# Layer norms taken apart by token chunk and woven into the blocks before and after them

## The chip, the cores and the metric

The kernel runs on one NeuronCore of a Trainium2 chip. The metric is the device time of one launch in microseconds (us). Five engines work side by side, each in its own program order: TensorE (PE in the profile) multiplies matrices, VectorE (DVE) and ScalarE (ACT) do elementwise work, GpSimd (POOL) and SyncE (SP) do the rest. They wait for one another through counting semaphores: `wait_ge(s, n)` holds an engine until `s` has reached `n`, and `.then_inc(s, 1)` raises `s` when an instruction has finished. A waiting engine runs nothing that stands behind the wait.

## The reference, cut to what matters

A two-layer decoder trunk works on 1024 prompt tokens and 8 sample tokens with a model width of 1024. Layer 0 has a Mamba-2 mixer, layer 1 a differential attention; each is followed by a squared-ReLU MLP, and after each of the four a layer norm closes the residual.

```python
def layer_norm(x, g, b):
    mu = jnp.mean(xf, -1, keepdims=True)
    var = jnp.mean(jnp.square(xf - mu), -1, keepdims=True)
    return ((xf - mu) * lax.rsqrt(var + LN_EPS) * g + b)

def sq_relu_mlp(x, w_up, w_down):
    return jnp.square(jax.nn.relu(x @ w_up)) @ w_down

for layer in range(2):
    y = mamba2_mixer(x, ...) if layer == 0 else diff_attention(x, ...)
    x = layer_norm(DN_ALPHA * x + y, ln_g[layer, 0], ln_b[layer, 0])
    x = layer_norm(DN_ALPHA * x + sq_relu_mlp(x, ...), ln_g[layer, 1], ln_b[layer, 1])
```

## The kernel before, in words

**Layout.** Activations lie transposed: 128 partitions hold one tile of features, 8 tiles (`k`) make the width of 1024, and the 1032 tokens run along the free dimension, cut into three token chunks (`c`) of 344. `acc` is the residual in float32. A matrix operand is kept as a high and a low part (`xh`/`xl`, `wh`/`wl`, `hh`/`hl`, `yh`/`yl`, `ah`/`al`), and a product is the sum of three matmuls.

**Jobs and units.** A job is one output tile of 128 features; its three chunks go into the three PSUM banks of `jb`. Weights come as units of 128x1024, loaded by SP and split by POOL into `wh` and `wl` in two slots. POOL may split into a slot once `unit_begun` shows that the unit that follows in the other slot has begun, for then the old one is finished. An ordinary `jobs` loop runs job by job and within it chunk by chunk, so a unit is used once and for one stretch. VectorE adds each finished bank to `acc` and frees it (`bank_free`); in the last block ahead of a layer norm (`accumulate_last`) it also sums the eight tiles into `ln0`, chunk by chunk of every job.

**The layer norm** has a part on three engines. PE: `mean` matmuls of `ln0` against a matrix of 1/1024 (line 493), then for each chunk the variance (24 small matmul instructions, line 499) and the spreading of the reciprocal roots over the partitions (6, line 506). DVE: centring (1316), the sum of the two halves of the squares (1320), the reciprocal (1324), scaling (1330), the low part (1337). ACT: squares (895), roots (899), the shifted high part (907). At the end DVE multiplies the residual by alpha in eight steps (1361). The order is written out by hand: all three means, then centre 0, centre 1, sum 0, centre 2 and so on, with two buffers for the squares (`lnq[:, c % 2]`). PE's order is variance and spread of chunks 0, 1 and 2, and only then the first matmul of the next stage (`jobs_after_norm`, line 532), which runs two jobs (`j` = 0, 1) chunk by chunk, 24 matmuls each, and waits for the low part of a whole chunk.

**After it.** In an MLP, ACT takes the relu out of a bank (942) and squares it (944), DVE squares it again and makes the low part (1373, 1375); there are four `rl` buffers, so the relu of the fifth chunk job waits for DVE's first (`h_ready`). After the second norm the first two jobs give query and key of head 0; DVE then forms lambda (from line 1399) and rotates them (1421) before the scores can begin (655).

**The four norms.** Norm 0 follows the mixer's last block (8 jobs of `yh`, two tiles deep, 6 matmuls a chunk job), norms 1 and 3 the last down block of an MLP (8 jobs, 12 matmuls a chunk job, 4 units), norm 2 the last attention projection (8 jobs, 3 matmuls a chunk job, one unit). After norm 3 the result is shifted and written out.

Of the kernel before, what the change touches and what calls it, by code (L numbers as in the profile page):

```python
# [110 lines left out]
def program(nc, a, o):  # L111
    with ExitStack() as ctx:
# [109 lines left out]
        m.close()  # L222

        m = ctx.enter_context(ExitStack())
        lnq = sb("lnq", [P, 2, KD, CW], F32, m)
# [87 lines left out]
        def _(pe):  # L313
# [170 lines left out]
            pe.wait_ge(s["y_lo"], 2 * GROUPS)  # L484
            jobs(Place(J_MLP0 - 8, U_MLP0 - 2), 8, 2, yh, yl)


            blocks = ((0, 0), (P, 0), (CW - P, 3 * P - CW))

            def layer_norm(l):  # L490
                for c in range(NCH):
                    pe.wait_ge(s["ln_sum"], 3 * l + c + 1)
                    mm(aux[:, c, 0:CW], ones[:, 0:P], ln0[:, c * CW:(c + 1) * CW], start=True, stop=True).then_inc(s["ln_mu"], 1)

                def variance(c):
                    pe.wait_ge(s["ln_add"], 3 * l + c + 1)
                    for b, (t0, _) in enumerate(blocks):
                        for k in range(4):
                            last = mm(aux[:, c, 500 + b:501 + b], lnq[:, c % 2, k, t0:t0 + P], ones[:, 0:1],  # L499
                                      start=(k == 0), stop=(k == 3))  # L500
                    last.then_inc(s["ln_var"], 1)

                def spread(c):
                    pe.wait_ge(s["ln_inv"], 3 * l + c + 1)
                    for b, (t0, skip) in enumerate(blocks):
                        last = mm(aux[:, c, t0 + skip:t0 + P], rstd[:, 1, 3 * c + b:3 * c + b + 1].to_broadcast([P, P]),  # L506
                                  ident[:, skip:P], start=True, stop=True)
                    last.then_inc(s["ln_scale"], 1)

                variance(0)  # L510
                spread(0)
                variance(1)
                spread(1)
                variance(2)
                spread(2)

            def jobs_after_norm(at, l):
# [3 lines left out]
                for c in range(NCH):  # L521
                    pe.wait_ge(s["ln_lo"], 3 * l + c + 1)
                    for j in range(2):
# [6 lines left out]
                        for k in range(KD):  # L530
                            for w, x, p in ((wh, xh, 0), (wh, xl, 1), (wl, xh, 2)):
                                last = mm(jb[:, bank, 0:CW], w[slot][:, k], x[:, k, cols],
                                          start=(k == 0 and p == 0), stop=(k == KD - 1 and p == 2))

                                if k == 0 and p == 0 and (c, j) in ((0, 0), (2, 1)):
                                    last.then_inc(unit_begun, 1)
                        last.then_inc(chunk_full, 1)

            def mlp(layer):
# [22 lines left out]
                down(at, 1, (hb + FFB) * 12)  # L562

            layer_norm(0)
            mlp(0)
            layer_norm(1)
# [8 lines left out]
            def project_head(at, n, new, fin):  # L575
# [51 lines left out]
                if fin:  # L627
# [96 lines left out]
            layer_norm(2)  # L724
            mlp(1)
            layer_norm(3)
# [3 lines left out]
        def _(act):  # L730
# [158 lines left out]
            def layer_norm(l):  # L889
                def squares(c, g):  # L890
                    act.wait_ge(s["ln_cent"], 6 * l + 2 * c + g + 1)
                    if c == 2:

                        act.wait_ge(s["ln_var"], 3 * l + 1)
                    af(lnq[:, c % 2, 4 * g:4 * g + 4], acc[:, 4 * g:4 * g + 4, c * CW:(c + 1) * CW], ACT.Square).then_inc(s["ln_sq"], 1)  # L895
# [31 lines left out]
                for c in (1, 2):  # L927
                    shift(c)

            def mlp(layer):  # L930
# [3 lines left out]
                def up(at, b, block_, order=UP_ORDER):  # L934
                    _, done = at.job(4)
                    for x, (j, c) in enumerate(order):
                        e = block_ * 12 + x

                        if not isinstance(e, int) or e >= 4:
                            act.wait_ge(s["h_ready"], e - 3)  # L940
                        act.wait_ge(chunk_full, done + x + 1)
                        af(rl[:, x % 4], jb[:, x % 3, 0:CW], ACT.Relu).then_inc(bank_free[x % 3], 1)  # L942
                        act.drain()
                        af(hh[b][:, j, c * CW:(c + 1) * CW], rl[:, x % 4], ACT.Square).then_inc(s["h_sq"], 1)  # L944

                up(Place(j0, 0), 0, hb, UP_ORDER_AFTER_NORM)
# [15 lines left out]
            layer_norm(0)  # L962
            mlp(0)
            layer_norm(1)
# [95 lines left out]
            for x, (j, c) in enumerate(UP_ORDER_AFTER_NORM[0:6]):  # L1060
                act.wait_ge(chunk_full, done + x + 1)
                af((raw, raw_k)[j][:, c * CW:(c + 1) * CW], jb[:, x % 3, 0:CW], ACT.Copy).then_inc(bank_free[x % 3], 1)
            act.drain().then_inc(s["raw_full"], 2)
# [15 lines left out]
            layer_norm(2)  # L1079
# [7 lines left out]
        def _(dve):  # L1087
# [51 lines left out]
            def accumulate_last(at):  # L1139

                for k in range(KD):
                    _, done = at.job()
                    for c in range(NCH):
                        cols = slice(c * CW, (c + 1) * CW)
                        dve.wait_ge(chunk_full, done + c + 1)
# [601 lines left out]
```

## Time and profile before

| | us |
|---|---|
| median of 3 runs (3884.25 to 3893.59) | 3885.5 |
| span of the profiled execution, first to last instruction | 3857.8 |
| TensorE busy in it | 3440.0 (89%) |
| VectorE / ScalarE / GpSimd busy | 2287.6 / 953.7 / 1011.1 |
| mean granted TensorE clock, share of full speed | 0.922 |

The profile is of one execution, and its span does not hold what lies around the first and last instruction, so the median stands 27.7 us above it. In timelines each row is a start, a length, the engine, the line of the kernel, the operation, what it writes and reads, its shape and how many instructions were merged; brackets tell how long the engine had been idle and whose work ended that.

### The profile page before, as it was taken

What the parts mean: (1) busy time and instruction counts of PE and PEld (TensorE: products, weight loads), DVE (VectorE), ACT (ScalarE), POOL (GpSimd) and SP (SyncE); (2) the same over time, 40 slices, a digit from 0 to 9 for tenths busy, and PEclk for the clock granted to TensorE, in tenths of its full rate; (3) what the DMA queues carried; (4) which work ended last, traced back from release to release, by engine and by line L of the source; (5) the groups of instructions that cost most, each with busy time, mean ns of one, the idle gap of its engine ahead of it and who ended that gap; (6) DMA issues with size and microseconds to landing.
All of it is one profiled execution on the core that took longest, in us unless ns stands there. A gap on an engine that the chain in (4) does not pass through costs nothing.

```text
span 3857.8 us, 55382 instructions
## 1 busy us (share of the span) xinstructions
PE 3440.0 (89%) x21050; PEld 3288.6 (85%) x21050; DVE 2287.6 (59%) x3463; ACT 953.7 (25%) x2235; POOL 1011.1 (26%) x455
## 2 busy tenths in 40 slices
PE   6888988889887899999997888888886799999997
PEld 6788888888787899999996787777775799999997
DVE  6677777777776834343457666666675753333335
ACT  3333333233332311111103323222322211111112
POOL 3123132222221233343431111111110043333331
PEclk9899999999998899999997888888897699999997
DMA  4231111111110011111112111211111011111111
GB/s 165 74 110 57 46 44 42 51 39 45 43 48 34 28 44 46 49 45 50 44 50 63 59 35 49 65 60 60 60 41 41 11 50 45 45 50 44 45 48 52
DMA packets 85936, 200.29 MB, mean 52 GB/s; under 512 B 8920, under 2 KB 46808, under 8 KB 85248
## 3 DMA queue, kind: packets, MB, share of 16 engines
q1 hardware_dynamic: 35552, 139.54, 10.8%
q10 hardware_dynamic: 50224, 58.37, 4.9%
q8 instruction: 131, 2.15, 0.2%
q14 instruction: 29, 0.24, 0.0%
HBM read 166.93 MB, written 39.60 MB: 54 GB/s over the span
## 4 chain that ended last, share of the span: by engine, by line
issue 65%; PE 19%; POOLq 9%; POOL 5%; SPq 1%; DVE 0%; ACT 0%; DMA 0%; ACTq 0%; DVEq 0%
PE jb L323 18%; POOLq L298 8%; POOL wl L299 5%; SPq L273 1%; PE aux L499 0%; DMA wraw<-in_wstream 0%; ACT acc L907 0%; DVE acc L1316 0%; POOLq L306 0%; POOLq L295 0%; SPq L263 0%; SPq L269 0%; DVE lnq L1320 0%; ACT lnq L895 0%; PE aux L506 0%
## 5 line engine op out<-in xcount | busy, mean ns | idle before, releaser
L296 POOL TENSOR_TENSOR wh<-wraw,one 128x1024 fp32r<-128x1024 f32 x225 | 444.5, 1976 | 2749.5 <-PE jb L323 2275.8
L323 PE MATMUL jb<-xh,wh 128*128 128x344 f32 x2784 | 912.7, 328 | 45.9 <-issue 18.6
L323 PE MATMUL jb<-xl,wh 128*128 128x344 f32 x2784 | 899.0, 323 | 0.0
L323 PE MATMUL jb<-xh,wl 128*128 128x344 f32 x2784 | 898.1, 323 | 0.0
L1132 DVE TENSOR_TENSOR acc<-jb,acc 128x344 f32<-128x344 f32 x672 | 332.1, 514 | 457.0 <-PE jb L323 446.3
L323 PEld LDWEIGHTS jb<-xh,wh 128*128 128x128 f32 x2784 | 532.0, 191 | 54.1 <-issue 22.8
L299 POOL TENSOR_TENSOR wl<-wraw,wh 128x1024 fp32r<-128x1024 f32 x225 | 566.3, 2517 | 32.0
L323 PEld LDWEIGHTS jb<-xl,wh 128*128 128x128 f32 x2784 | 531.5, 191 | 1.6
L323 PEld LDWEIGHTS jb<-xh,wl 128*128 128x128 f32 x2784 | 531.2, 191 | 0.0
L323 PE MATMUL jb<-hh,wh 128*128 128x344 f32 x1536 | 492.3, 321 | 0.0
L323 PE MATMUL jb<-hl,wh 128*128 128x344 f32 x1536 | 491.0, 320 | 0.0
L323 PE MATMUL jb<-hh,wl 128*128 128x344 f32 x1536 | 490.5, 319 | 0.0
L1373 DVE TENSOR_TENSOR rl<-rl 128x344 f32<-128x344 f32 x192 | 158.1, 823 | 371.7 <-ACT hh L944 371.5
L942 ACT ACTIVATE rl<-jb 128x344 f32<-128x344 f32 x192 | 87.8, 457 | 1072.7 <-PE jb L323 1045.7
L323 PEld LDWEIGHTS jb<-hh,wh 128*128 128x128 f32 x1536 | 288.8, 188 | 3.4 <-DVE acc L1132 3.4
L323 PEld LDWEIGHTS jb<-hh,wl 128*128 128x128 f32 x1536 | 288.6, 188 | 0.0
L323 PEld LDWEIGHTS jb<-hl,wh 128*128 128x128 f32 x1536 | 288.1, 188 | 0.0
L1375 DVE TENSOR_TENSOR hl<-rl,hh 128x344 fp32r<-128x344 f32 x192 | 228.4, 1190 | 15.8 <-issue 2.0
L1163 DVE SCALAR_TENSOR_TENSOR ct<-pre,pg,ct 128x1024 f32<-128x1024 f32 x96 | 165.3, 1722 | 99.4 <-ACT cnew L813 90.6
L323 PE MATMUL jb<-yh,wh 128*128 128x344 f32 x384 | 136.8, 356 | 69.0 <-DVE acc L1132 51.7
L1034 ACT ACTIVATE pp<-aux,st 128x256 f32<-128x256 f32 (+7 forms) x128 | 94.1, 739 | 280.4 <-PE jb L666 158.1
L323 PEld LDWEIGHTS jb<-yh,wh 128*128 128x128 f32 x384 | 79.2, 206 | 79.5 <-DVE acc L1132 60.2
(247 smaller groups left out, 5662.9 us busy)
## 6 DMA issues: line engine op xcount, KB each, us to landing
wraw<-in_wstream SPq DMA_DIRECT2D x225, 512.0 KB, 3.3
kgat<-in_cache_k SPq DMA_DIRECT2D x16, 512.0 KB, 5.2
vgat<-in_cache_v SPq DMA_DIRECT2D x16, 512.0 KB, 6.1
pre<-in_state ACTq DMA_DIRECT2D x16, 512.0 KB, 4.2
out_ssm_s<-pre ACTq DMA_DIRECT2D x16, 512.0 KB, 3.5
past<-kgat ACTq DMA_DIRECT2D x8, 1024.0 KB, 5.9
past<-vgat ACTq DMA_DIRECT2D x8, 1024.0 KB, 5.9
acc<-in_xT SPq DMA_DIRECT2D x8, 516.0 KB, 7.0
```

Of the source, the lines that this page charges most:

```text
L273: pages = [sp.value_load(a["ptab"][0:1, k:k + 1], min_val=0, max_val=PHYS - 1) for k in range(NB * PAGES)]
L296: nc.gpsimd.tensor_tensor(wh[slot][:].rearrange("p k m -> p (k m)"), wraw[:, slot].rearrange("p k m -> p (k m)"), one[:].to_broadcast([P, ...
L298: pool.drain()
L299: nc.gpsimd.tensor_tensor(wl[slot][:], wraw[:, slot], wh[slot][:].bitcast(F32), ALU.subtract).then_inc(w_split, 1)
L323: last = mm(jb[:, c, 0:CW], w[slot][:, j * kt + k], x[:, k, cols], start=(k == 0 and p == 0), stop=(k == kt - 1 and p == 2))
L942: af(rl[:, x % 4], jb[:, x % 3, 0:CW], ACT.Relu).then_inc(bank_free[x % 3], 1)
L1034: af(pp[:, m_ * 1024:m_ * 1024 + width], src, ACT.Exp, scale=SCALE, bias=st[:, m_:m_ + 1], accum_out=st[:, 2 + m_:3 + m_]).then_inc(s["p_r ...
L1132: tt(acc[:, k, cols], jb[:, c, 0:CW], acc[:, k, cols], ALU.add).then_inc(bank_free[c], 1)
L1163: stt(ct[:, 0:SEQ], src[:, 1 + k:1 + k + SEQ], w(k), ct[:, 0:SEQ], ALU.mult, ALU.add)
L1373: tt(rl[:, x % 4], rl[:, x % 4], rl[:, x % 4], ALU.mult)
L1375: tt(hl[b][:, j, cols], rl[:, x % 4], f(hh[b][:, j, cols]), ALU.subtract).then_inc(s["h_ready"], 1)
```

## The change

Three things are rearranged for each norm. (1) The last block runs chunk by chunk: all jobs of chunk 0, then of chunk 1, then of chunk 2 (`jobs_by_chunk`, `accumulate_by_chunk`); in an MLP in two calls of four jobs, each of which holds two weight units until its third chunk. The mean of chunk 0 is issued behind chunk 1's jobs, that of chunk 1 behind chunk 2's. DVE centres chunk 0 behind its adds of chunk 1, sums chunk 0's squares in the middle of chunk 2, and centres chunk 1 behind chunk 2. (2) Behind the block PE does variance 0, mean 2 and spread 0, and then goes to the first jobs of the next stage; variance and spread of chunks 1 and 2 stand there, each ahead of its chunk's two jobs. (3) DVE alternates scaling and low part tile by tile, PE waits for the low part of each tile (`24 * l + 8 * c + k + 1`) and not of a chunk, ACT takes the first two results (`first_out`) between the shifts of chunk 1 and the root of chunk 2. There is one buffer of squares in place of two, in memory of its own.

```diff
+            def jobs_by_chunk(at, n, kt, rh, rlo, norm=None, low=None):
+                slots = []
+                per = 8 // kt
+                credits, _ = at.job(n)
                 for c in range(NCH):
...
+                    for j in range(n):
+                        if c == 0 and j % per == 0:
+                            slots.append(unit(at))
+                        x = c * n + j
+                        bank = x % 3
+                        pe.wait_ge(bank_free[bank], credits + x // 3)
...
+                                if k == 0 and p == 0 and (c, j) in ((0, 0), (NCH - 1, per)):
+                                    last.then_inc(unit_begun, 1)
+                        last.then_inc(chunk_full, 1)
+                    if norm is not None and c:
+                        mean(norm, c - 1)
+
+            def layer_norm_end(l):
+                variance(l, 0)
+                mean(l, 2)
+                spread(l, 0)
 
             def jobs_after_norm(at, l):
...
                 for c in range(NCH):
-                    pe.wait_ge(s["ln_lo"], 3 * l + c + 1)
+                    if c:
+                        variance(l, c)
+                        spread(l, c)
                     for j in range(2):
...
                         for k in range(KD):
+                            if j == 0:
+                                pe.wait_ge(s["ln_lo"], 24 * l + 8 * c + k + 1)
...
-                down(at, 1, (hb + FFB) * 12)
-            layer_norm(0)
+                pe.wait_ge(s["h_ready"], (hb + FFB) * 12)
+                jobs_by_chunk(at, 4, 4, hh[1], hl[1])
+                jobs_by_chunk(at, 4, 4, hh[1], hl[1], 2 * layer + 1)
+                layer_norm_end(2 * layer + 1)
```

ScalarE:

```diff
-                for c in (0, 1):
-                    for g in (0, 1):
-                        squares(c, g)
+                for g in (0, 1):
+                    squares(0, g)
                 root(0)
+                for g in (0, 1):
+                    squares(1, g)
+                shift(0)
                 root(1)
                 for g in (0, 1):
                     squares(2, g)
-                shift(0)
+                shift(1)
+                if first_out:
+                    first_out(0)
+                    first_out(1)
                 root(2)
...
-                for c in (1, 2):
-                    shift(c)
+                shift(2)
```

VectorE:

```diff
+            def accumulate_by_chunk(at, n, k0, l=None):
+                _, done = at.job(n)
+                for c in range(NCH):
...
+                    for j in range(n):
...
+                        if l is not None and c == 2 and j == n // 2 - 1:
+                            add_squares(l, 0)
+                    if l is not None and c:
+                        centre(l, c - 1)
...
                 def scale(c):
                     dve.wait_ge(s["ln_scale"], 3 * l + c + 1)
                     for k in range(KD):
                         v = acc[:, k, c * CW:(c + 1) * CW]
                         stt(v, v, lnp[:, l, 0, k:k + 1], aux[:, c, 0:CW], ALU.mult, ALU.mult).then_inc(s["ln_norm"], 1)
+                        if l < 3 and k > 1:
+                            low(c, k - 2)
...
                 drain()
-                centre(0)
-                centre(1)
-                add_squares(0)
-                centre(2)
+                add_squares(l, 1)
                 invert_root(0)
-                add_squares(1)
-                drain()
                 scale(0)
+                centre(l, 2)
                 invert_root(1)
-                add_squares(2)
-                low(0)
+                scale(1)
+                add_squares(l, 2)
                 invert_root(2)
-                scale(1)
-                low(1)
                 scale(2)
-                low(2)
```

## Rows read from the trace of the kernel before

**Rows 1.** Timeline of PE through norm 1, from its means to the next stage.

```profile
2026.06 2.22 PE L493 MATMUL aux<-ln,ones 128*128 128x344 f32 x6
2035.11 5.28 PE L499 MATMUL aux<-ones,lnq 128*128 128x1 f32 x24 [6.83 <-DVE lnq L1320]
2040.95 1.58 PE L506 MATMUL aux<-ident,rstd 128*128 128x128 f32 x6 [0.57 <-DVE rstd L1324]
...
2059.31 0.63 PE L532 MATMUL jb<-xh,wh 128*128 128x344 f32 x1
```

**Rows 2.** Timeline of PE: last matmul of norm 1's first jobs, first scores.

```profile
2083.85 0.32 PE L532 MATMUL jb<-xl,wh 128*128 128x344 f32 x1
2084.01 0.32 PE L532 MATMUL jb<-xh,wl 128*128 128x344 f32 x1
...
2112.58 0.44 PE L655 MATMUL aux<-k2h,q 128*128 128x128 f32 x1 [8.62 <-DMA k2l<-k2l]
```

**Rows 3.** Timeline of DVE through norm 1.

```profile
2026.86 0.52 DVE L1151 TENSOR_TENSOR ln<-ln,acc 128x344 f32<-128x344 f32 x1
2027.47 6.08 DVE L1316 TENSOR_TENSOR acc<-acc,aux 128x1376 f32<-128x1376 f32 x4
2033.47 1.58 DVE L1320 TENSOR_TENSOR lnq<-lnq 128x1376 f32<-128x1376 f32 x1
...
2042.58 3.96 DVE L1330 SCALAR_TENSOR_TENSOR acc<-acc,lnp,aux 128x344 f32<-128x344 f32 x8 [0.20 <-PE aux L506]
...
2052.03 3.98 DVE L1337 SCALAR_TENSOR_TENSOR xl<-acc,lnp,xh 128x344 fp32r<-128x344 f32 x8
...
2061.71 6.14 DVE L1337 SCALAR_TENSOR_TENSOR xl<-acc,lnp,xh 128x344 fp32r<-128x344 f32 x8
```

**Rows 4.** Timeline of ACT through norm 1.

```profile
2029.09 5.84 ACT L895 ACTIVATE lnq<-acc 128x1376 f32<-128x1376 f32 x4 [92.62 <-DVE acc L1316]
2040.43 0.26 ACT L899 ACTIVATE rstd<-aux,eps 128x3 f32<-128x3 f32 x1 [5.49 <-PE aux L499]
```

**Rows 5.** Timeline of PE in the mixer: 18 one-column matmul instructions between dense jobs.

```profile
482.92 2.06 PE L377 MATMUL aux<-ones,zs 128*128 128x1 f32 x18
```

**Rows 6.** Stretches: length, busy of each engine, granted clock (PEclk), DMA share, GB/s.

```profile
2031.00:2061.60 30.60, 22.49 (x98) 21.89 (x99) 22.15 (x34) 11.50 (x18) 1.57 (x1) 0.50 0.10 34
...
3024.30:3037.90 13.60, 8.84 (x33) 4.64 (x31) 12.49 (x24) 0.56 (x1) 0.00 (x0) 1.00 0.01 1
```

**Rows 7.** Timeline of PE in the last blocks ahead of norms 0 and 2.

```profile
1246.96 0.43 PE L323 MATMUL jb<-yh,wh 128*128 128x344 f32 x1 [1.11 <-DVE acc L1146]
...
3025.78 0.42 PE L323 MATMUL jb<-ah,wh 128*128 128x344 f32 x1 [0.29 <-DVE acc L1146]
```

**Rows 8.** Timelines of PE and POOL where norm 0's first jobs end.

```profile
1319.69 0.42 PE L323 MATMUL jb<-xh,wh 128*128 128x344 f32 x1 [1.23 <-POOL wl L299]
...
1314.94 2.09 POOL L296 TENSOR_TENSOR wh<-wraw,one 128x1024 fp32r<-128x1024 f32 x1 [16.24 <-PE jb L532]
1317.17 2.46 POOL L299 TENSOR_TENSOR wl<-wraw,wh 128x1024 fp32r<-128x1024 f32 x1
```

**Rows 9.** Timelines of DVE and ACT behind norms 0 and 1.

```profile
1309.86 5.42 DVE L1361 TENSOR_SCALAR acc<-acc,lnp 128x1032 f32<-128x1032 f32 x8
...
1320.04 0.46 ACT L942 ACTIVATE rl<-jb 128x344 f32<-128x344 f32 x1 [8.06 <-DVE hl L1375]
...
2086.51 0.16 DVE L1407 TENSOR_TENSOR lam<-lam 128x1 f32<-128x1 f32 x1 [3.04 <-ACT lam L1066]
```

**Rows 10.** Timeline of DVE in the attention: one step with POOL busy, then with POOL idle.

```profile
2814.97 0.85 DVE L1550 TENSOR_SCALAR pp<-pp,st,lam 128x384 f32<-128x384 f32 x1
...
2927.46 0.48 DVE L1550 TENSOR_SCALAR pp<-pp,st,lam 128x384 f32<-128x384 f32 x1
```

**Rows 11.** Timelines of PE and ACT in norm 3: first mean, last shift.

```profile
3810.82 2.23 PE L493 MATMUL aux<-ln,ones 128*128 128x344 f32 x6
...
3847.82 3.88 ACT L907 ACTIVATE acc<-acc,lnp 128x344 f32<-128x344 f32 x8 [0.66 <-DVE acc L1330]
```

More of the change, by code:

```diff
@@ new lines, in mean, with variance @@
+            def mean(l, c):
+                pe.wait_ge(s["ln_sum"], 3 * l + c + 1)
+                mm(aux[:, c, 0:CW], ones[:, 0:P], ln0[:, c * CW:(c + 1) * CW], start=True, stop=True).then_inc(s["ln_mu"], 1)
+            def variance(l, c):
+                pe.wait_ge(s["ln_add"], 3 * l + c + 1)
+                for b, (t0, _) in enumerate(blocks):
+                    for k in range(4):
+                        last = mm(aux[:, c, 500 + b:501 + b], lnq[:, k, t0:t0 + P], ones[:, 0:1],
+                                  start=(k == 0), stop=(k == 3))
+                last.then_inc(s["ln_var"], 1)
@@ new lines, in spread @@
+            def spread(l, c):
+                pe.wait_ge(s["ln_inv"], 3 * l + c + 1)
+                for b, (t0, skip) in enumerate(blocks):
+                    last = mm(aux[:, c, t0 + skip:t0 + P], rstd[:, 1, 3 * c + b:3 * c + b + 1].to_broadcast([P, P]),
+                              ident[:, skip:P], start=True, stop=True)
+                last.then_inc(s["ln_scale"], 1)
+            def jobs_by_chunk(at, n, kt, rh, rlo, norm=None, low=None):
+                slots = []
+                per = 8 // kt
+                credits, _ = at.job(n)
+                for c in range(NCH):
+                    if low is not None:
+                        pe.wait_ge(s["a_lo"], 3 * low + c + 1)
+                    for j in range(n):
[4 more added lines that the diff above has]
+                        pe.wait_ge(bank_free[bank], credits + x // 3)
+                        for k in range(kt):
+                            for w, r, p in ((wh, rh, 0), (wh, rlo, 1), (wl, rh, 2)):
+                                last = mm(jb[:, bank, 0:CW], w[slots[j // per]][:, (j % per) * kt + k], r[:, k, c * CW:(c + 1) * CW],
+                                          start=(k == 0 and p == 0), stop=(k == kt - 1 and p == 2))
+                                if k == 0 and p == 0 and (c, j) in ((0, 0), (NCH - 1, per)):
[3 more added lines that the diff above has]
+                        mean(norm, c - 1)
@@ L626, in project_head @@
                     rms_spread(p, "orms_scale", "orms_inv")
-                if fin:
+                if fin and not new:
+                    jobs_by_chunk(at, KD, 1, ah, al, 2, p)
+                    layer_norm_end(2)
+                elif fin:
                     slot = unit(at)
@@ L722, in _ @@
             project_head(Place(J_MLP1 - 8, U_MLP1 - 1), HEADS_B, False, True)
-            layer_norm(2)
             mlp(1)
-            layer_norm(3)
+            for c in (1, 2):
+                variance(3, c)
+                spread(3, c)
         @block.scalar
@@ L926, in layer_norm, with up_chunk @@
                     act.dma_start(lamv, a["lamv"].partition_broadcast(P)).then_inc(s["attc_in"], 16)
-                for c in (1, 2):
-                    shift(c)
+                shift(2)
+            def up_chunk(done, b, block_, x, j, c):
+                e = block_ * 12 + x
+                if not isinstance(e, int) or e >= 4:
+                    act.wait_ge(s["h_ready"], e - 3)
+                act.wait_ge(chunk_full, done + x + 1)
+                af(rl[:, x % 4], jb[:, x % 3, 0:CW], ACT.Relu).then_inc(bank_free[x % 3], 1)
+                act.drain()
+                af(hh[b][:, j, c * CW:(c + 1) * CW], rl[:, x % 4], ACT.Square).then_inc(s["h_sq"], 1)
             def mlp(layer):
@@ L932, in mlp, with up, first_up @@
                 hb = layer * FFB
-                def up(at, b, block_, order=UP_ORDER):
+                def up(at, b, block_):
                     _, done = at.job(4)
[L936 to L946, printed above, removed]
+                    for x, (j, c) in enumerate(UP_ORDER):
+                        up_chunk(done, b, block_, x, j, c)
+                _, done = Place(j0, 0).job(4)
+                def first_up(x):
+                    up_chunk(done, 0, hb, x, *UP_ORDER_AFTER_NORM[x])
+                layer_norm(2 * layer, first_up)
+                for x in range(2, 12):
+                    first_up(x)
                 with act.Fori(0, FFB // 2 - 1) as i:
@@ L1077, in _ @@
             project_head(Place(J_MLP1 - 8, 0), HEADS_B, False, True)
-            layer_norm(2)
             mlp(1)
```

95 lines of the change are left out of this document (36 added, 59 removed).

## The prediction

> **What bounds the kernel now.** I read the page first (PE is busy 89% of the span), then PE's timeline at each of the four norms, where PE has its long holes, then DVE's and ACT's timelines beside it. In norm 1 the last matmul of the block ends at 2026.2, the first of the next stage starts at 2059.31 [rows 1] and the last of the first two jobs ends at 2084.33 [rows 2]: 58.1 us, of which 144 matmuls at 0.157 us start to start (24 in 3.77 us; two starts in [rows 2]) need 22.6. So a norm costs PE about 35 us. The chain inside is serial: DVE centres, ACT squares, DVE adds, PE takes the variance, ACT the root, DVE the reciprocal, PE spreads, DVE scales [rows 1, 3, 4]. Through all of it the granted clock is 0.50, the 1.2 GHz level [rows 6]; the 24 variance instructions take 5.28 us there, while 18 of their kind take 2.06 between dense jobs in the mixer [rows 5], so 24 would take 2.75. The blocks ahead of norms 0 and 2 are paced by DVE, for which PE waits 1.11 and 0.29 us at a bank [rows 7]; the MLP blocks are paced by PE.
>
> **The steps of a chunk after the change.** From the start of a chunk's scaling DVE alternates scale and low, 8 steps each in 3.96 and 3.98 [rows 3], 0.49 a step. The first low part is done behind three scales, at 2.0 us, the eighth at 7.9, and PE's last three matmuls of the first job end at 8.4: this job is paced by DVE and not by PE. The second job adds 3.77. Then PE does the variance of the next chunk, 2.75 at the high clock or 5.28 at the low one; root and reciprocal 0.57, spread 1.58 or about half of it [rows 1]. I take 2.75 and 1.2, since the second job is dense, and the granted clock is 1.00 even in a stretch of norm 2's block where three matmuls come with each pair of DVE's adds, 1.04 us (24 adds in 12.49, [rows 6, 7]). One chunk then costs 2.75 + 0.57 + 1.2 + 0.1 + 8.4 + 3.77 = 16.8 us (19.7 if all is at the low clock), and nothing of the next chunk can begin in it on PE, because variance and spread stand behind both jobs in PE's order. The first chunk has no variance in it, but POOL splits a unit meanwhile; DVE's low parts with two SBUF inputs are held up by that (eight took 6.14 and not 3.98, [rows 3]), and with scales in between I count 2.7: 8.4 + 2.7 + 3.77 = 14.9.
>
> **From the last sum of the block to the end of the first jobs.** Before, in norm 1: 2027.38 to 2084.33 [rows 2, 3], 56.9. After: centre 1 takes 3.08 (half of 6.08), the second half of the squares 1.35 (ACT's four took 5.84 with waits between), their sum 1.58 [rows 3, 4], reciprocal and spread 1.9: scaling starts at 7.9; + 14.9 + 2 x 16.8 = 56.4. So the first matmul comes some 18 us earlier and the last at the same time: half a us is won. If variance 0 comes late (it stands behind the block's last job, and with one buffer the squares of chunk 1 wait for it), 1.1 to 3.6 are lost; that holds in norms 0 and 2, where DVE is not behind PE's last job by more than a us.
>
> **What moves into the blocks.** Centre 0 (3.08) and sum 0 (1.58) now stand in DVE's order among the adds. Norm 2's block is paced by DVE [rows 7]: + 4.7, - 0.5, + 2.3 = **+6.5** (5 to 9). Norm 0's block has holes at its cold start that hide part: **+4.5** (2.5 to 8). In norms 1 and 3 PE's block is longer than DVE's work, 7.5 us a chunk, but DVE's last chunk then holds 3.08 + 1.58 + 4.1 of adds, behind a lag of 1.2, and in norm 1 two POOL operations of the split hold it up: the last sum comes 3.7 later: norm 1 **+3.2** (0 to 9). Norm 3 has no next stage and no further unit: scaling 0 starts 10.3 behind the block, then scale 3.96, centre 3.08, reciprocal and spread 1.86, scale 3.96, sum 1.5, variance 5.28 (here PE is idle and the clock low), 0.57 and 1.58, scale and shift 4.5, in all 36.7; before, the last shift ended at 3851.7, 40.7 behind the block [rows 11]: **-4.0** (-5 to 0).
>
> **Weights.** A call that pins both slots to its third chunk frees the first unit only 24 matmuls before the next call wants a unit. Norm 0's first jobs already show this: PE had 24 matmuls, 3.77, against a split of 2.09 + 2.46 and its latencies, and waited 1.23 for POOL [rows 8]. After, this happens three times in each MLP's last block (second unit of the first call, both of the second): 6 x 1.23 = **+7.4** (4 to 9). SP's loads of the raw weights stay ahead, since a slot of `wraw` is freed as before by the split.
>
> **Behind the norms.** DVE's last low part now ends 4.3 ahead of the first jobs' end and not 8.6. The eight alpha steps (5.42, [rows 9]) so fall into POOL's split of the next unit, which starts 3.4 ahead of that end; before, they had just ended [rows 8, 9]. A DVE step of one SBUF input and two scalars took 0.85 with POOL busy and 0.48 without [rows 10]; no row shows the alpha step itself so. If each split lets only two DVE steps through, alpha ends 3 to 4 later again. DVE's first low part of the MLP, which releases ACT's fifth relu at 1320.04 [rows 9], 1.6 behind the first jobs' end at 1318.46 [rows 8], then comes at 1.6 + 4.3 + 3.4 = 9.3; PE's eighth chunk job, due at 1.23 + 3.77 behind that end, wants the bank that this relu empties 0.5 later: 9.8 - 5.0, less 0.4 because the seventh job starts a little late as well, 4.4 each in two MLPs, **+8.8** (0 to 16, with a fallen clock). Behind norm 1 the rotation for head 0 waits for the same steps and for ACT's exponential; 3.04 of DVE's delay are hidden there [rows 9], the scores wait for DVE's chain [rows 2]: 4.3 + 4.2 (both operations of a split, 2.09 + 2.46, less the work they let through) - 3.0 + 1 for the later exponential, **+6.5** (1 to 9). The page "SBUF — State Buffer" of the Trainium skill, section "Who interferes with whom", states that a `tensor_scalar` in a two-port mode and a GpSimd instruction shut each other out for the whole instruction; by that rule the alpha steps are held up in full, which is the 3 to 4 us that the sum has, and without it about 7 us of the 34 would be gone. That speaks against this change; the trace agrees for the attention step, 0.85 against 0.48.
>
> **The sum.** 4.5 + 3.2 + 6.5 - 4.0 + 7.4 + 8.8 + 6.5 = 32.9 on a span of 3857.8 us (the table), 3890.7; the 27.7 around it are unchanged, so 3885.5 + 32.9 = 3918 us for the median.
>
> **Rivals.** (A) The forecast: serial chunk, pinned weights, DVE late: 3918. (B) The same serial chunk, but DVE's lateness stays hidden (POOL and alpha don't collide, four `rl` buffers suffice): 4.5 + 3.2 + 6.5 - 4.0 + 7.4 = 17.6, and nothing behind the norms: 3903. For it: before, ACT waited 8.06 for DVE [rows 9] and PE not at all. (C) The clock stays low through the woven stage, as it did in the norm [rows 6]: six chunks at 19.7 and not 16.8 add 17.4: 3936. Against it: the dense second jobs. (D) Not slower: the clock never falls, because PE is never idle for as long as now. Then norm 3's reductions run at the high clock (2 x 2.5 + 3 x 0.8 less, 7), norms 0 to 2 save up to 0.4 in each of six chunks and 2.5 on variance 0 (7), and DVE, in time, costs nothing behind: 17.6 - 14, and from the point at which DVE also starts chunk 0 without the 2.7 and the 3.7 of hold-ups (12), it is -8: 3877. Against it: 8.4 of each chunk is DVE's pace, whatever the clock. (E) The weaving does nothing: each norm's first reduction still ends where it did and the chunks cost what they cost; only the pinned weights are left: 3893.
>
> **How the numbers follow.** A 0.52, B 0.22, C 0.08, D 0.1, E 0.08. A measurement can tell about 0.3%, 11.7 us. A, B and C are slower by more than that (the low tail of B, 0.05, is not); E is within; D is half within and half faster. Slower 0.77, within 0.18, faster 0.05. The range runs from 3889, which leaves out D and part of E, to 3945, the sum with every term at its upper bound (8 + 9 + 9 + 0 + 9 + 16 + 9 = 60); all terms of A at their lower bounds give 7.5, 3893.
>
> **What would show it.** In the changed profile: the first matmul of the next stage 14 to 17 us behind the block and not 33; between the three pairs of first jobs two holes of about 7 us with variance and spread in them, the variance near 2.75; three waits of 1.2 for POOL in each MLP's last block; alpha steps much longer than 0.75; a wait of PE for ACT's relu behind norms 0 and 2; the rotation of head 0 later by some 6. It would be wrong if variance and spread came while PE still had jobs to do, if alpha ran through POOL's split unhindered, or if norm 3 gained much more than 4.

## The result and the profile of the changed kernel

| | before | changed |
|---|---|---|
| median of the device time | 3884.9 us (3874.8 to 3893.6) | 3939.0 us (3936.8 to 3941.7) |
| ratio, 95% interval | | 1.016 (1.0127 to 1.0194) |
| profiled execution: its own time, its span | about 3859.6 (below), 3857.8 | 3940.4, 3938.6 |

The changed kernel is slower by 54 us. The forecast had the sign and most of the mechanism, but 33 us; the range (3889 to 3945) holds the time.

Between the two profiles the spans differ by 80.8 us and not by 54. Before any of that is put down to the change, the profile of before has to be looked at again. I cut both executions into nine stages at the same instructions of PE: the first matmul of the block ahead of a norm, the last matmul of the first jobs behind it, the last matmul of an MLP, the first scores. The third line is a second profile of the unchanged kernel, from the first experiment:

```
us              mixer   norm 0  MLP 0   norm 1  head 0  heads   norm 2  MLP 1   norm 3   span
before         1229.6    88.82  707.76   58.11   28.25  896.6    83.40  718.40   46.79  3857.8
before again   1237.6    88.87  707.71   58.10   28.29  927.6    83.40  718.05   46.78  3896.4
changed        1239.1    94.15  719.90   64.83   34.55  924.6    89.47  730.22   41.79  3938.6
```

The seven stages that the prediction costs are the same to 0.4 us in both profiles of before. The mixer and the heads, which the change does not touch, are not: they differ by 39 us between two executions of one kernel. Against the second profile the changed kernel differs by +5.3, +12.2, +6.7, +6.3, +6.1, +12.2 and -5.0 in the seven stages, in all **+43.7**, and by -1.5 in the other two together.

Norm 1 in the changed kernel, the timeline of PE (start, duration, line, operation, in brackets the idle time ahead of it and what ended it):

```profile
2056.06 3.47 PE L491 MATMUL aux<-ones,lnq 128*128 128x1 f32 x24 [2.33 <-DVE lnq L1192]
...
2064.22 1.58 PE L498 MATMUL aux<-ident,rstd 128*128 128x128 f32 x6 [3.33 <-DVE rstd L1374]
2068.02 0.63 PE L552 MATMUL jb<-xh,wh 128*128 128x344 f32 x1 [2.21 <-DVE xl L1379]
...
2071.05 0.65 PE L552 MATMUL jb<-xh,wh 128*128 128x344 f32 x1 [0.92 <-DVE xl L1379]
...
2073.63 0.65 PE L552 MATMUL jb<-xh,wh 128*128 128x344 f32 x1 [1.36 <-DVE xl L1379]
...
2082.21 2.73 PE L491 MATMUL aux<-ones,lnq 128*128 128x1 f32 x24
2085.51 1.58 PE L498 MATMUL aux<-ident,rstd 128*128 128x128 f32 x6 [0.57 <-DVE rstd L1374]
2089.30 0.63 PE L552 MATMUL jb<-xh,wh 128*128 128x344 f32 x1 [2.21 <-DVE xl L1379]
...
2100.05 2.93 PE L491 MATMUL aux<-ones,lnq 128*128 128x1 f32 x24
2103.55 1.58 PE L498 MATMUL aux<-ident,rstd 128*128 128x128 f32 x6 [0.57 <-DVE rstd L1374]
2107.66 0.62 PE L552 MATMUL jb<-xh,wh 128*128 128x344 f32 x1 [2.52 <-DVE xl L1379]
...
2117.67 0.32 PE L552 MATMUL jb<-xh,wl 128*128 128x344 f32 x1
```

The block ends at 2053.2. The first matmul of the next stage comes 14.9 us behind it, as the prediction's 14 to 17, and not 33.1 [rows 1], but the last one 64.8 behind it and not 58.1 [rows 2]: what is won at the front is spent behind it. Twice PE goes through variance, root, spread and the wait for the first low part before the next pair of jobs (7.1 us from 2082.21, 7.6 from 2100.05), and the three pairs of jobs take 35.3 us together, where before they took 25.0 in one row. The granted clock in three stretches of this norm (length, busy time of PE, PEld, DVE, ACT, POOL, granted clock, DMA share, GB/s):

```profile
2058.10:2078.50 20.40, 12.57 (x41) 9.99 (x41) 17.31 (x22) 7.32 (x11) 4.34 (x2) 0.50 0.08 27
2085.40:2095.60 10.20, 7.88 (x26) 6.83 (x27) 8.52 (x18) 7.47 (x12) 0.00 (x0) 0.50 0.00 1
2102.50:2112.70 10.20, 7.11 (x25) 5.97 (x25) 7.48 (x16) 4.91 (x10) 0.00 (x0) 0.50 0.39 132
```

It is 0.50, the 1.2 GHz level, at the start of each chunk, behind the idle time of PE, and rises within the pair of jobs. Variance 1 and 2, at the end of a pair, take 2.73 and 2.93 and not 5.28 [rows 1].

Behind norm 0, DVE's alpha steps (one group: shortest, median and longest duration in ns, first and last start), POOL's casts of two weight units beside them, ACT's fifth relu, and PE:

```profile
L1407 DVE TENSOR_SCALAR acc<-acc,lnp x8: 746/1569/2851, 1328.8 to 1340.9; 128x1032 f32<-128x1032 f32 x8
```

```profile
1329.73 2.23 POOL L293 TENSOR_TENSOR wh<-wraw,one 128x1024 fp32r<-128x1024 f32 x1 [39.60 <-PE jb L552]
1332.10 2.63 POOL L296 TENSOR_TENSOR wl<-wraw,wh 128x1024 fp32r<-128x1024 f32 x1
1335.30 2.41 POOL L293 TENSOR_TENSOR wh<-wraw,one 128x1024 fp32r<-128x1024 f32 x1 [0.57 <-PE jb L320]
1337.84 2.62 POOL L296 TENSOR_TENSOR wl<-wraw,wh 128x1024 fp32r<-128x1024 f32 x1
```

```profile
1342.90 0.46 ACT L968 ACTIVATE rl<-jb 128x344 f32<-128x344 f32 x1 [13.22 <-DVE hl L1421]
...
1334.78 0.43 PE L320 MATMUL jb<-xh,wh 128*128 128x344 f32 x1 [1.53 <-POOL wl L296]
...
1343.41 0.66 PE L320 MATMUL jb<-xh,wh 128*128 128x344 f32 x1 [4.59 <-ACT rl L968]
```

The eight steps take 12.90 us from 1328.78 (5.42 before [rows 9]): four take 0.75 and four 2.4 to 2.85; these end 0.55 behind the end of one of POOL's instructions each, so each waits out one of them. ACT waits 13.2 us for DVE and PE 4.59 for ACT. PE's clock falls to 0.50 behind that:

```profile
1333.20:1341.20 8.00, 4.10 (x25) 3.77 (x24) 8.00 (x5) 0.00 (x0) 6.56 (x3) 1.00 0.19 66
1341.30:1348.00 6.70, 4.58 (x16) 4.59 (x17) 6.18 (x14) 2.83 (x6) 0.00 (x0) 0.50 0.24 78
```

16 matmuls take 4.58 us there; at the 0.157 from start to start of [rows 2] they need 2.5, so 2.1 us more are lost. All waits of PE in MLP 0 (total, times, longest):

```profile
PE jb L320 <- ACT rl L968: 4.6, 1, 4.6
PE jb L518 <- POOL wl L296: 3.0, 3, 1.0
PE jb L320 <- issue: 2.2, 2, 1.3
PE jb L320 <- POOL wl L296: 1.5, 1, 1.5
```

MLP 1 has the same four groups (`issue` comes to 8.7 there, as it does before the change). Norm 3, from PE's first mean of it to ACT's last shift:

```profile
3896.64 0.74 PE L485 MATMUL aux<-ln,ones 128*128 128x344 f32 x2
3897.22 2.73 PE L491 MATMUL aux<-ones,lnq 128*128 128x1 f32 x24
...
3928.57 3.97 ACT L935 ACTIVATE acc<-acc,lnp 128x344 f32<-128x344 f32 x8 [2.49 <-DVE acc L1386]
```

The last shift ends 35.7 behind the block (3896.81) and not 40.7 [rows 11].

### The profile page after: what moved, and what is told of

The parts are those of the page before. It is cut to its first block, busy times and chain, and to the rows that moved or that the text cites. A ratio compares the mean times of both kernels' runs of the same rounds, so it can differ in the third digit from the quotient of the medians.

```text
span 3938.6 us, 55378 instructions
## 1 busy us (share of the span) xinstructions
PE 3473.9 (88%) x21050; PEld 3311.5 (84%) x21050; DVE 2296.1 (58%) x3463; ACT 960.0 (24%) x2235; POOL 1011.8 (26%) x455
## 3 DMA queue, kind: packets, MB, share of 16 engines
q1 hardware_dynamic: 35552, 139.54, 10.2%
## 4 chain that ended last, share of the span: by engine, by line
issue 78%; POOLq 12%; POOL 7%; SPq 1%; DVE 1%; PE 1%; DMA 0%; ACT 0%; DVEq 0%
POOLq L295 11%; POOL wl L296 7%; SPq L270 1%; PE jb L518 0%; DMA wraw<-in_wstream 0%; DVE acc L1386 0%; POOLq L303 0%; POOLq L292 0%; DVE acc L1188 0%; PE aux L491 0%; PE aux L498 0%; DVE lnq L1192 0%; SPq L260 0%; ACT acc L935 0%; SPq L266 0%
## 5 line engine op out<-in xcount | busy, mean ns | idle before, releaser
L320 PE MATMUL jb<-hh,wh 128*128 128x344 f32 x1344 | 430.9, 321 | 0.0
L320 PE MATMUL jb<-hl,wh 128*128 128x344 f32 x1344 | 429.6, 320 | 0.0
L320 PE MATMUL jb<-hh,wl 128*128 128x344 f32 x1344 | 429.1, 319 | 0.0
L320 PEld LDWEIGHTS jb<-hh,wh 128*128 128x128 f32 x1344 | 252.7, 188 | 3.4 <-DVE acc L1177 3.4
L320 PEld LDWEIGHTS jb<-hh,wl 128*128 128x128 f32 x1344 | 252.5, 188 | 0.0
L320 PEld LDWEIGHTS jb<-hl,wh 128*128 128x128 f32 x1344 | 252.1, 188 | 0.0
L320 PE MATMUL jb<-yh,wh 128*128 128x344 f32 x336 | 120.0, 357 | 58.3 <-DVE acc L1177 51.6
L701 PE MATMUL aux<-wt,vth 128*128 128x256 f32 x288 | 92.7, 346 | 55.0 <-DVEq L1579 54.8
```

The source lines that it names most:

```text
L320: last = mm(jb[:, c, 0:CW], w[slot][:, j * kt + k], x[:, k, cols], start=(k == 0 and p == 0), stop=(k == kt - 1 and p == 2))
L701: last = mm(aux[:, 4, 0:256], vv[:, k], wt[:, k].rearrange("p a b -> p (a b)"), start=(k == 0 and p == 0), stop=(k == i and p == 1))
```

## The experiments

Where an experiment changes the order only, the stages tell more than the whole time, since the mixer and the heads differ between executions by more than the edits. The seven stages of each (sum of the seven, and that less the 1731.2 of "before again"):

```
us                  norm 0  MLP 0   norm 1  head 0  norm 2  MLP 1   norm 3     sum   more
changed              94.15  719.90   64.83   34.55   89.47  730.22   41.79  1774.9  +43.7
alpha later          94.14  711.88   66.21   28.34   89.08  720.87   41.78  1752.3  +21.1
variance between     89.61  720.12   59.62   35.63   83.99  728.71   41.78  1759.5  +28.3
units free           94.15  717.34   64.28   35.66   91.38  728.97   41.78  1773.6  +42.4
all three            90.69  709.53   57.96   28.23   84.64  718.77   41.80  1731.6   +0.4
before, norm 3 only  87.54  708.54   58.12   28.32   83.41  720.20   41.80  1727.9   -3.3
before, alpha later  87.38  707.76   58.10   28.36   83.05  717.51   46.81  1729.0   -2.2
```

Stages that an edit does not touch stay within 2 us of where they were; that is what a difference in one stage has to exceed.

**The kernel before, again.** No edit.

> The kernel before, unchanged, profiled and timed anew. Of the 54 us by which the changed kernel is longer, the stages that the prediction costed hold 43 between the two profiles, and another 38 lie in the mixer and the heads, which the change does not touch: the head's period is 112.6 us in most heads of the profile of before and 119.5 in most of the changed kernel's. Theory 1: the period is a matter of the execution, the profile of before was a fast one of its kernel, and the 27.7 us that the prediction took for time around the span were time that other executions spend in the heads. Then this profile or its times show it: either a span near 3875 to 3884 with most heads at 119, or again a span near 3858 with its execution's own time only about 2 us above it, some 25 below the median. Theory 2: the changed kernel itself drives the heads into the longer period and some 25 us really lie around the span of before. Then the heads are at 112.6 again and the execution's own time stands some 25 us above its span.

Measured: 3894.2 us median, 3856.7 to 3898.2 in 12 runs (ratio 1.0019, 0.9984 to 1.0054); the profiled execution took 3898.21 us with a span of 3896.4. One head of the first profile in which the period is long, one in which it is short, and one of the second profile (columns as above):

```profile
2348.80:2466.80 118.00, 100.32 (x576) 92.36 (x576) 76.11 (x134) 33.82 (x71) 17.20 (x8) 0.84 0.17 53
2692.20:2804.80 112.60, 95.77 (x575) 88.19 (x574) 75.79 (x134) 33.82 (x71) 17.22 (x8) 0.89 0.18 56
```

```profile
2700.00:2819.50 119.50, 101.68 (x574) 93.74 (x574) 76.30 (x134) 33.85 (x71) 17.22 (x8) 0.83 0.17 53
```

The same work, the same instructions, but the granted clock is 0.89 on the mean in the short heads and 0.83 to 0.84 in the long ones. The first profile has 112.6 to 112.7 in its last four periods, the second none. Theory 1 holds, though the span lies 12 us above the one that it named: a profiled execution takes 1.8 us more than its span (3898.21 against 3896.4 here, 3940.39 against 3938.6 in the changed kernel), so the first profile's took about 3859.6, 25 us less than its median.

**Alpha steps later.** VectorE's eight steps on acc behind norms 0 to 2 move behind later work:

```diff
-                    for k in range(KD):
-                        ts(acc[:, k], acc[:, k], lnp[:, l, 1, k:k + 1], ALPHA, ALU.add, ALU.mult)
-                    drain()
...
                         tt(hl[b][:, j, cols], rl[:, x % 4], f(hh[b][:, j, cols]), ALU.subtract).then_inc(s["h_ready"], 1)
+                        if norm is not None and x >= 4:
+                            alpha(norm, x - 4)
...
+                if isinstance(n, int) and n == 0:
+                    alpha(1, 2 * j)
+                    alpha(1, 2 * j + 1)
                 dve.wait_ge(s["qk_hi"], 2 * e)
...
+                        for k in range(4, KD):
+                            alpha(1, k)
```

> The changed kernel with one thing moved: the eight steps by which VectorE multiplies acc by alpha (the ones on 128x1032, 12.9 us each behind a norm in the trace of the changed kernel, 5.4 in the trace of before) no longer run in one row right behind the norm, ahead of the first unit of the next block, but one by one between later steps of VectorE: in the MLPs behind the last eight chunks of the first up block, in layer 1 between the rope steps of head 0. Nothing is left out. Theory (the steps stand in the way of the shift of the first h chunks, which TensorE waits for): TensorE's wait of 4.58 us for ScalarE behind the first jobs of either MLP goes, with it the stretch at half clock that follows it (some 2 us), and head 0's first scores come some 8 us earlier; in all about -20 us (3919). Rival (the wait is owed to the order of the weights and first jobs, the alpha steps only lie beside it): under 5 us.

Measured: 3916.6 us median (ratio to before 1.0067, 1.0018 to 1.0117). The stages: MLP 0 -8.0, MLP 1 -9.4, head 0 -6.2, norm 1 +1.4. PE's waits in MLP 0 of this kernel, and the stretch in which the changed kernel's clock was at 0.50 (8.0 to 14.8 us behind the first jobs):

```profile
PE jb L518 <- POOL wl L296: 3.0, 3, 1.0
PE jb L320 <- issue: 1.6, 2, 0.9
PE jb L320 <- POOL wl L296: 1.0, 1, 1.0
```

```profile
1336.40:1343.20 6.80, 6.80 (x45) 6.80 (x44) 6.58 (x11) 1.90 (x4) 1.97 (x1) 1.00 0.14 49
```

The wait for ACT and the fall of the clock are gone, and the rival (under 5 us) with them. DVE there, with POOL's casts at 1324.82 to 1326.74, 1326.88 to 1329.33, 1329.90 to 1331.89 and 1332.03 to 1334.52:

```profile
1324.47 0.52 DVE L1420 TENSOR_TENSOR hl<-rl,hh 128x344 fp32r<-128x344 f32 x1
1324.90 2.21 DVE L1418 TENSOR_TENSOR rl<-rl 128x344 f32<-128x344 f32 x1
1327.19 2.52 DVE L1420 TENSOR_TENSOR hl<-rl,hh 128x344 fp32r<-128x344 f32 x1
...
1336.43 0.75 DVE L1407 TENSOR_SCALAR acc<-acc,lnp 128x1032 f32<-128x1032 f32 x1
```

POOL now holds up the steps on `rl` and `hl`, 2.0 to 2.7 us and not 0.52, while alpha behind the casts takes 0.75. It costs PE nothing here, because the first `hl`, for which ACT's fifth relu waits, starts ahead of the first of these casts and is done at 1325.0, and the first jobs end only at 1328.4.

**Variance between the first jobs.** On TensorE only:

```diff
                 for c in range(NCH):
-                    if c:
-                        variance(l, c)
-                        spread(l, c)
                     for j in range(2):
+                        if c < NCH - 1 and j:
+                            variance(l, c + 1)
+                            spread(l, c + 1)
```

> The changed kernel with variance and spread of token chunk c+1 put between the two first jobs of chunk c on TensorE, in place of ahead of chunk c+1. Nothing is left out. Theory (the chunk of 16.6 to 17.9 us is a chain: jobs, then variance, ScalarE's root, spread, scaling and only then the next jobs, TensorE idle in it): the period falls to about 13 us, which is -3.8 for each of two chunks in each of three norms, in all -18 to -23 us (about 3918). Rival (the chunk is set by VectorE's scaling of 8 tiles, or by the 12 us of the jobs with the waits for their low parts): the period stays over 16 and the time within 4 us of the changed kernel's.

Measured: 3921.8 us median (ratio to before 1.0101, 1.0064 to 1.0137); norm 0 -4.5, norm 1 -5.2, norm 2 -5.5, in all -15.2. The three spreads of norm 1:

```profile
2055.20 1.58 PE L498 MATMUL aux<-ident,rstd 128*128 128x128 f32 x6 [4.15 <-DVE rstd L1374]
...
2074.97 1.58 PE L498 MATMUL aux<-ident,rstd 128*128 128x128 f32 x6 [0.56 <-DVE rstd L1374]
...
2089.41 0.90 PE L498 MATMUL aux<-ident,rstd 128*128 128x128 f32 x6 [0.57 <-DVE rstd L1374]
```

From spread to spread 19.8 and 14.4, against 21.3 and 18.0 in the changed kernel. So the order of PE, and not DVE's scaling, sets the chunk: the theory holds in kind. Its 13 us were too little; the first variance now runs ahead of the second job, at the low clock (5.11 us at 2069.29), and gives part of it back.

**Job order in the first half of the last block.** In each MLP only the last four jobs go by chunk:

```diff
-                jobs_by_chunk(at, 4, 4, hh[1], hl[1])
+                jobs(at, 4, 4, hh[1], hl[1])
...
-                accumulate_by_chunk(at, 4, 0)
+                accumulate_half(at)
```

(`accumulate_half` does the adds of these four jobs in the order by job, as `accumulate_last` did in the kernel before.)

> The changed kernel with the first four jobs of each MLP's last block in the order by job again (all three chunks of a job, then the next job, as in the kernel before); only the last four go chunk by chunk. Nothing is left out. Theory (the chunk order asks for all weight units of the block at its start, and the casts on GpSimd come 0.9 to 1.5 us late for each): the waits for the weights' low part in the last block fall from three to one in either MLP, which is 2 us each, in all -4 us (3935). Rival (the forecast's price of 1.2 us for each of six late weights, 7.4 in all, is right and the jobs' order sets it): -7. Second rival (the waits move to the last four jobs): no change.

Measured: 3941.4 us median (ratio to before 1.0142, 1.0095 to 1.0189), no difference that can be told from the changed kernel. The waits fall as the theory says; MLP 0:

```profile
PE jb L518 <- POOL wl L296: 1.0, 1, 1.0
```

One wait and not three, and the MLPs are shorter by 2.6 and 1.3. But norm 2, which the edit does not touch, is 1.9 longer here, and head 0 1.1. Alone, the run shows the waits and no time. Beside the alpha steps it shows more: from "alpha later" to "all three" the MLPs become shorter by 2.4 and 2.1.

**All three edits.** The three diffs above in one kernel:

```diff
+                            alpha(norm, x - 4)
...
+                            variance(l, c + 1)
+                            spread(l, c + 1)
...
+                jobs(at, 4, 4, hh[1], hl[1])
```

> The changed kernel with all three edits at once: alpha steps later, variance and spread between the two first jobs, and the first four jobs of the MLPs' last blocks job by job. Nothing is left out. Theory (the three costs are separate stretches, so their gains add): from the stages of the single edits, norm 0 89.6, MLP 0 about 709.5, norm 1 about 60, head 0 28.3, norm 2 84, MLP 1 about 719, norm 3 41.8, which is -38 to -42 against the changed kernel and +1 against the kernel before (between -2 and +4). Rival (the edits hand their waits to one another: a norm that ends earlier meets the same split of the weights): each MLP keeps 3 us or more over its 707.7 and 718.1 of before, and the whole stays 8 or more above the kernel before.

Measured: 3879.8 us median beside 3876.3 for before (ratio 1.0014, 0.9984 to 1.0044); the seven stages stand +0.4 above before. PE's waits in MLP 0:

```profile
PE jb L320 <- issue: 1.8, 2, 1.1
PE jb L320 <- POOL wl L296: 1.0, 1, 1.0
PE jb L518 <- POOL wl L296: 1.0, 1, 1.0
```

The gains add: -22.6, -15.4 and -1.4 would give +4.3, and +0.4 is there. The 43.7 are 48.7 us of costs less the 5.0 that norm 3 wins. The three edits take out 43.3 of the 48.7, in their order of size: alpha steps that come late and run into POOL's casts, a chunk that is serial on PE, and weight slots that are held too long. The rival (3 us or more left in each MLP) falls with 1.8 and 0.7. Freed of them, the weave of norms 0 to 2 wins nothing: 1.8 and 1.2 over before in norms 0 and 2, -0.1 in norm 1.

**Only norm 3 woven, on the kernel before.** TensorE's part (ScalarE and VectorE follow it, for this norm alone):

```diff
-                down(at, 1, (hb + FFB) * 12)
+                if layer == 0:
+                    down(at, 1, (hb + FFB) * 12)
+                else:
+                    pe.wait_ge(s["h_ready"], (hb + FFB) * 12)
+                    jobs(at, 4, 4, hh[1], hl[1])
+                    last_block(at)
```

> The kernel before with only norm 3 woven into the last four jobs of its block, as the changed kernel does it; norms 0 to 2 and the stages behind them are as before. Nothing is left out. Theory (the weave gains where no stage follows, since there is nothing to hold up): norm 3 goes from 46.8 to 41.8 us, MLP 1 gains at most one wait for weights, 1 us; in all -4 to -5 (0.1%), all other stages within 0.5 us of before. Rival (the 5 us are won because the changed kernel's block hands VectorE an earlier start by its order in both halves): -1 to -2.

Measured: 3886.6 us median, 3847.1 to 3895.9 (ratio to before 1.0000, 0.9962 to 1.0038). Norm 3 takes 41.80, -5.0 as in the changed kernel, but MLP 1 takes 2.2 longer, where at most 1 was expected; half of it is a wait that the kernel before does not have:

```profile
PE jb L531 <- POOL wl L300: 1.1, 1, 1.1
```

-2.8 us for both stages is 0.07% and not the -4 to -5 expected; norm 0, which the edit does not touch, is 1.3 shorter. The gain in norm 3 is clear in the profile, the whole is below what the times can tell: by its stages this is the best version here, and no time confirms it.

**Alpha steps later, on the kernel before.** The same edit as in the second experiment, without the weave:

```diff
+                        if norm is not None and x >= 4:
+                            alpha(norm, x - 4)
```

> The kernel before with only the alpha steps moved, to the places that they took in the second experiment. Nothing is left out. Theory (the steps hurt only because the weave brings VectorE to them later, into GpSimd's split of the next weights): norms, MLPs and head 0 within 1 us of the kernel before. Rival (the move is a gain of its own, and what it gave in the second experiment is no price of the weave): 5 us or more less in each MLP or in head 0.

Measured: 3894.6 us median (ratio 1.003, 0.9999 to 1.0062); MLP 0 +0.1, MLP 1 -0.5, head 0 +0.1 against "before again" (norm 0, which had to stay within 1 us, -1.5). The move is worth nothing on its own in the stages that it touches; the 23.6 us that it gave in MLPs and head 0 were the price of the weave.

## Why the prediction was right or wrong

The terms, forecast and as the stages measure them:

| term | forecast | measured | |
|---|---|---|---|
| norm 0 | +4.5 | +5.3 | right |
| norm 1 | +3.2 | +6.7 | too small: the clock |
| norm 2 | +6.5 | +6.1 | right |
| norm 3 | -4.0 | -5.0 | right |
| weights, both MLPs | +7.4 | about +7.6 | right |
| behind the norms, both MLPs | +8.8 | about +16.8 | the wait right by two errors, the fall of the clock left out |
| head 0 | +6.5 | +6.3 | right sum, wrong parts |
| sum | +32.9 | +43.7 | |

**The step that failed: the clock.** The sum takes TensorE's clock as high wherever dense jobs stand ("since the second job is dense"). The runs show the granted clock at 0.50 at the start of each chunk of norm 1, which costs most of the 3.5 us that this norm lacks, and at 0.50 behind PE's wait for ACT, which costs 2.1 us in each MLP and stood in the range but not in the sum. That is some 7 of the 10.8 us by which the terms are short. (That the clock was 0.50 "through all of" the old norm was read from 30.6 of its 58.1 us [rows 6].)

**Chunk.** The forecast of 16.8 us holds where variance and spread run as assumed: in norms 0 and 2 the second and third spread stand 16.8 apart, with variances of 2.73 and spreads of 0.9 to 1.24. (The clock is at 0.50 there as well, for 6.8 us, but within the first job, which DVE paces.) In norm 1 they are 18.0 apart: from the spread on the clock is 0.50 for 10.2 us, the spread took 1.58 and not 1.2, and the jobs behind it started at that level. The first chunk was sized at 14.9 with 2.7 for POOL's hold-up. The hold-up came as forecast (two low parts take 1.75 and 2.18, the others 0.57), but the chunk takes 16.4, because the matmuls behind PE's waits of 0.92 and 1.36 run at the 0.50 that the forecast had high. Rival C (3936) comes nearest to the time but not by its mechanism: the clock does rise in each pair of jobs. C was also worked out too low: its 19.7 leaves the second job at 3.77, where 24 matmuls at the low level need 6.9 (16 take 4.58 behind norm 0).

**Weights.** Three waits in each last block, as forecast. PE stands idle for 0.9 to 1.1 at each and not 1.23, but counted from matmul to matmul each costs 1.2 to 1.3, about 7.6 for the six.

**Behind the norms: the term that was mis-sized.** The forecast has the chain right: alpha late, DVE's `hl` late, ACT's fifth relu late, PE short of a bank. Its times came out as well: the relu 9.3 behind the first jobs, and it comes 9.65 behind them (1342.90 against 1333.25); PE's wait 4.4, and PE waits 4.59. But that is luck in part. "If each split lets only two DVE steps through, alpha ends 3 to 4 later again" counted one split. Two follow one another with 0.57 between them: two alpha steps run free, four wait for one POOL instruction each, and the two others run in the gap between the two splits and behind the last. 12.90 - 5.42 = 7.5 is twice 3.7. The second split stood in the trace of before, too, 0.56 behind the first [rows 8]. There alpha had ended, and the first `rl` and `hl` steps met the casts (first two fences, before); in the changed kernel they run free (third fence):

```profile
1320.20 1.99 POOL L296 TENSOR_TENSOR wh<-wraw,one 128x1024 fp32r<-128x1024 f32 x1 [0.56 <-PE jb L323]
```

```profile
1315.36 2.05 DVE L1373 TENSOR_TENSOR rl<-rl 128x344 f32<-128x344 f32 x1
1317.47 2.53 DVE L1375 TENSOR_TENSOR hl<-rl,hh 128x344 fp32r<-128x344 f32 x1
```

```profile
1341.76 0.52 DVE L1419 TENSOR_TENSOR rl<-rl 128x344 f32<-128x344 f32 x1
1342.35 0.52 DVE L1421 TENSOR_TENSOR hl<-rl,hh 128x344 fp32r<-128x344 f32 x1
```

From the start of this `rl` to the end of this `hl` it took 4.65 before and 1.11 after, so 3.5 of the 7.5 were moved and not added. What the sum lacked lies behind the wait. Counted from matmul to matmul against "before again", MLP 0's 12.2 us are 4.75 for the wait for ACT, 2.1 for the low clock behind it, 3.8 for the weights, 0.7 for the mean that now stands in the last block and 0.9 in two short waits; MLP 1's come out alike. Against the 4.4 forecast the alpha edit gave 8.0 and 9.4 back, since it takes out the wait, the low clock and part of the short waits together; about 1 us of the 9.4 lies far behind, in the loop of MLP 1. The Trainium skill's page "SBUF — State Buffer", section "Who interferes with whom", says that whichever of a two-port DVE step and a GpSimd instruction comes first keeps the port pair for its whole length; the durations of 0.75 or 2.4 to 2.85, with nothing between, agree. The same section says that a DVE step with two SBUF inputs contends with a GpSimd instruction that reads SBUF; the `rl` and `hl` steps of 2.0 to 2.7 in the second experiment agree.

**Head 0.** +6.5 came out as 6.3 by two errors that cancel. The alpha steps lasted 7.5 longer (12.95 at 2113.45) and not 4.2. But POOL's hold-up was partly moved and not added: before, it held up the rotation behind alpha, and after, the rotation runs free:

```profile
2087.26 2.94 DVE L1421 TENSOR_TENSOR rot<-raw,cos 128x1032 f32<-128x1032 f32 x1
...
2091.58 1.97 DVE L1426 TENSOR_TENSOR rot<-rot,raw 128x1032 f32<-128x1032 f32 x1
```

```profile
2113.45 12.95 DVE L1407 TENSOR_SCALAR acc<-acc,lnp 128x1032 f32<-128x1032 f32 x8
...
2129.59 1.23 DVE L1468 TENSOR_TENSOR rot<-raw,cos 128x1032 f32<-128x1032 f32 x1
```

The first of these fences is the kernel before, the second the changed one. The rotation starts 11.6 behind the end of the first jobs (2118.0) and not 2.9 behind it (2084.3), 8.7 later, and then wins 2.5 back in the two steps that took 2.94 and 1.97 before.

**The base.** "The 27.7 around it are unchanged" was wrong. The profile and the three times of before were set side by side as if they were one execution; the difference was taken for time outside the span. Outside the span lie 1.8 us. The rest was four heads of 112.6 us in one profiled execution, where the second profile has 119.5, and a mixer 8.0 us shorter. What should have raised the doubt stood in the trace: heads that do the same work at two periods. Built on an execution whose heads are all long, the sum is 3898.2 + 43.7 = 3941.9, 3 above the median measured. So of the 21 us between forecast and median, 11 are the terms and 10 the base: as far as times and clocks on record tell, the median of before is pulled down by executions with some short heads. Of 28 further executions of before, ten took under 3865 us at a mean granted clock of 0.923 to 0.927, the others 3886 to 3903 at 0.910 to 0.916; the four of the changed kernel (3936.8 to 3941.7, at 0.910 to 0.912) give no sign of short heads.

## What to carry to other kernels

Interleaving a chain with dense work costs time where the dense engine's own order keeps that work out of the chain's gaps: here variance and spread were queued behind both jobs, and swapping them with one job gave back 15 of 44 us. Even with all three edits the weave of norms 0 to 2 won nothing. Look for what a moved step now lies beside, instruction by instruction: four of eight short steps of 0.75 us took 2.4 to 2.9, because they came 4 us later against two weight casts that had been there before as well, and that held PE behind ScalarE behind VectorE. A wait of a dense engine can cost more than its length: 4.6 us of waiting for ScalarE, and 2.1 more at half the clock behind it. And set the profiled execution against its own time before its span is used as a base.

## What the runs showed of the hardware that was not expected

An unchanged kernel has two periods for its heads, 112.6 and 119.5 us, with nearly the same waits of PE (16.8 and 17.8 us in a period) and a mean granted clock of 0.89 or 0.83. Executions of the kernel before run from 3847 to 3904 us; seven periods of 6.9 us would be 48 of these 57. And one execution can pass from one period to the other, as the first profile does behind its third head (119.5, then 118.0, then 112.7). It is not the unchanged kernel alone: the profile of "all three" has 119.5, 117.9, 112.8, 112.7 and then 117.1, so an execution can leave the short period again. What decides it stays open: none of the 21 runs of the changed kernel, of "variance between" and of "units free" was below 3915, two of 12 of "alpha later" were (3864 and 3872, against 3914 to 3924), and none of 10 of "before, alpha later" was below 3888, though its heads are those of before. No run here was made to settle that.
